# Scores of both kv heads issued in turn, and the projection of the 64 sample rows with high and low feature parts side by side

## What is computed

```python
xn = rmsnorm(x, p["attn_norm_w"])
proj = xn @ p["w_in"]                 # q, k, v, mq, mk, mv, mo, mi, mf, ga, gb
q = rmsnorm(q.reshape(B, T, N_KV_HEADS, G, HEAD_DIM), ...) * (HEAD_DIM ** -0.5)
k = rmsnorm(k.reshape(B, T, N_KV_HEADS, HEAD_DIM), ...)
...
s = jnp.einsum("bnqhgd,bnkhd->bnhgqk", q, k)     # per block of 128 queries: its own and the previous key block
...
p = jnp.exp(s - m)
den = p.sum(axis=-1, keepdims=True) + jnp.exp(sink - m)
return jnp.einsum("bnhgqk,bnkhd->bnqhgd", (p / den), v)
```

## Time and profile before

| | |
|---|---|
| median of 3 runs | 1626.4 us (1626.13 to 1628.06) |
| the profiled execution | 1630.05 us, span 1628.2 us |
| TensorE matmuls busy | 1465.9 us, 90% |
| VectorE busy | 986.0 us, 61% |
| ScalarE busy | 739.1 us, 45% |
| mean granted TensorE clock | 0.955 of full speed |
| `project`: first to last of its matmuls | 21.1 to 314.7 us |
| `mix_prompt`: its first gate matmul | 322.6 us |

### The profile page before, as it was taken

One profiled execution on the slowest core, in us unless ns is written; L12 is line 12 of the kernel. 1 busy time (PEld: TensorE's weight loads), 2 busy tenths in 40 slices (PEclk: granted clock), 3 DMA queues, 4 the chain that ended last, 5 costly groups with the idle time before them and its releaser, 6 DMA issues. The chain is left out here.

```text
span 1628.2 us, 22132 instructions
## 1 busy us (share of the span) xinstructions
PE 1465.9 (90%) x8287; PEld 1254.0 (77%) x8287; DVE 986.0 (61%) x1316; ACT 739.1 (45%) x869; POOL 203.8 (13%) x233
## 2 busy tenths in 40 slices
PE   6999999789999999789989947999999999999960
PEld 5999999788999999778868835777777777777740
DVE  4422311135555555657556665888888888888845
ACT  6321120134444444332132105777777777777732
POOL 2600000001111111200020002211111111111003
PEclk9999999889999999899999967999999999999985
DMA  6222228333333321646751055999999999999818
GB/s 219 74 74 74 73 77 259 104 109 96 96 95 95 95 89 54 168 136 179 229 224 71 33 219 183 382 385 403 390 393 388 401 395 389 388 400 397 311 64 326
DMA packets 135556, 347.54 MB, mean 213 GB/s; under 512 B 13528, under 2 KB 91804, under 8 KB 109824
## 3 DMA queue, kind: packets, MB, share of 16 engines
q1 hardware_dynamic: 125224, 312.11, 52.8%
q0 software_dynamic: 6160, 21.89, 4.4%
q10 hardware_dynamic: 4120, 12.85, 2.0%
HBM read 292.91 MB, written 54.89 MB: 214 GB/s over the span
## 5 line engine op out<-in xcount | busy, mean ns | idle before, releaser
L455 PE MATMUL pj<-w_hi,f_hi 128*128 128x352 f32 (+3 forms) x576 | 187.7, 326 | 4.7 <-ACTq L171 4.7
L456 PE MATMUL pj<-w_lo,f_hi 128*128 128x352 f32 (+3 forms) x576 | 187.1, 325 | 0.0
L457 PE MATMUL pj<-w_hi,f_lo 128*128 128x352 f32 (+3 forms) x576 | 186.8, 324 | 0.0
L2077 DVE TENSOR_TENSOR e_w_lo<-mixed,e_w_hi 128x2048 fp32r<-128x2048 f32 x64 | 145.7, 2296 | 11.7 <-ACT e_w_hi L2009 11.7
L2077 DVE TENSOR_TENSOR e_w_lo<-w_out,e_w_hi 128x2048 fp32r<-128x2048 f32 x64 | 143.5, 2283 | 0.0
L870 PE MATMUL gate_banks<-f_hi,wg_hi 128*128 128x364 f32 (+1 forms) x384 | 130.7, 340 | 10.3 <-PEq L93 7.6
L2009 ACT CAST e_w_hi<-mixed 128x2048 fp32r<-128x2048 f32 x64 | 120.2, 1906 | 37.7 <-PEq L93 21.2
L871 PE MATMUL gate_banks<-f_lo,wg_hi 128*128 128x364 f32 (+1 forms) x384 | 127.1, 331 | 0.0
L872 PE MATMUL gate_banks<-f_hi,wg_lo 128*128 128x364 f32 (+1 forms) x384 | 126.9, 331 | 0.0
L2009 ACT CAST e_w_hi<-w_out 128x2048 fp32r<-128x2048 f32 x64 | 121.7, 1902 | 1.7 <-PE e_up L2147 1.7
L455 PEld LDWEIGHTS pj<-w_hi,f_hi 128*128 128x128 f32 (+1 forms) x576 | 105.4, 183 | 7.4 <-ACTq L171 5.6
(11 more groups left out here) (496 smaller groups left out, 3393.8 us busy)
## 6 DMA issues: line engine op xcount, KB each, us to landing
w_out<-in_w_down_e SPq DMA_DIRECT2D x64, 1024.0 KB, 8.9
mixed<-in_w_gate_e SPq DMA_DIRECT2D x32, 1024.0 KB
mixed<-in_w_up_e SPq DMA_DIRECT2D x32, 1024.0 KB, 9.2
w_gate<-in_w_gate_e SPq DMA_DIRECT2D x32, 1024.0 KB, 7.6
w_up<-in_w_up_e SPq DMA_DIRECT2D x32, 1024.0 KB, 8.9
expert_rows<-e_y_rows ACTq DMA_DIRECT2D x32, 384.0 KB, 7.4
proj<-mixed SPq DMA_DIRECT2D x8, 1408.0 KB, 6.1
proj_tile<-proj SPq DMA_DIRECT2D x8, 1408.0 KB, 6.2
```

What stands on the lines that cost most here:

```text
L455: pe.matmul(banks[b][:r, :w], hi, w_hi[v][:, k, 0:w], start=(k == 0), stop=False)
L456: pe.matmul(banks[b][:r, :w], hi, w_lo[v][:, k, 0:w], start=False, stop=False)
L457: ins = pe.matmul(banks[b][:r, :w], lo, w_hi[v][:, k, 0:w], start=False, stop=(k == KD - 1))
L2077: dve.tensor_tensor(lo(i, u, j), raw(i, u, j), hi(i, step, j).bitcast(F32), ALU.subtract).then_inc(lo_ready[i], 1)
```

## The change

In `project` the sample tile gets a second copy of its features (`side`): per block k 128 stationary columns, the high part in the first 64 and the low part in the last 64. One matmul of it with the high weights gives high times high in the upper half of the bank's partitions and low times high in the lower half; the matmul of the high features with the low weights (64 columns) is added to the upper half as before. The two halves are added afterwards: ScalarE copies partitions 64 to 127 to `stage`, then VectorE adds partitions 0 to 63 (`add_sample`), frees the bank and counts `staged` up, for which `store` now waits. In `mix_prompt` the score matmuls alternate between the two kv heads, both counts of `sc_full` come at the end, and the waits for `mqT` and `mkT` stand in front of the first score.

```diff
+        side = [nc.alloc_sbuf_tensor_at("f_side0", [P, KD - 1, P], F32R, offset=nc.sbuf_base - 4 * (3 * D - 2 * T)),
+                nc.alloc_sbuf_tensor_at("f_side1", [P, 1, P], F32R, offset=S["mixed_at"] + 4 * (2 * half + 2 * T))]
...
-                    copy(stage[v][:r, t, :], banks[b][:r, :CW]).then_inc(done, 1)
+                    at = slice(TS, P) if t == NT else slice(0, r)
+                    copy(stage[v][:r, t, :], banks[b][at, :CW]).then_inc(done, 1)
...
-                    eng.wait_ge(done, per * cc + t // 2 + 1)
-                    eng.sem_inc(free[b], 1)
+                    if t < NT:
+                        eng.wait_ge(done, per * cc + t // 2 + 1)
+                        eng.sem_inc(free[b], 1)
+
+            def add_sample(dve, n):
+
+                cc, v = n // 2, n % 2
+                b = 3 * v + NT % 3
+                dve.wait_ge(staged[0][v], 5 * cc + 5)
+                dve.tensor_tensor(stage[v][:TS, NT, :], stage[v][:TS, NT, :], banks[b][:TS, :CW], ALU.add).then_inc(staged[1][v], 1)
+                if n == 0:
+                    dve.wait_ge(if_staged[0], 5)
+                    held = if_tok[:TS, NT, :].rearrange("p (g c) -> p g c", g=2)[:, :, 0:H]
+                    dve.tensor_tensor(held, held, banks[b][:TS, CW:CW + 2 * H].rearrange("p (g c) -> p g c", g=2), ALU.add).then_inc(if_staged[1], 1)
+                    dve.wait_ge(if_staged[1], 5)
+                dve.wait_ge(staged[1][v], 5 * cc + 5)
+                dve.sem_inc(free[b], 1)
...
                 def store(n):
                     cc, v = n // 2, n % 2
                     sp.wait_ge(staged[0][v], 5 * cc + 5)
-                    sp.wait_ge(staged[1][v], 4 * cc + 4)
+                    sp.wait_ge(staged[1][v], 5 * cc + 5)
...
                 def feat_hi(t, r):
                     act.wait_ge(featT_ready, t + 1)
-                    act.copy(feat(f_hi, t, r), f_tile[t % 2][:, :, 0:r]).then_inc(f_hi_ready, 1)
+                    ins = act.copy(feat(f_hi, t, r), f_tile[t % 2][:, :, 0:r])
+                    if t == NT:
+                        act.wait_ge(f_lo_ready, NT)
+                        for ks in (slice(0, KD - 1), slice(KD - 1, KD)):
+                            ins = act.copy(f_side(ks)[:, :, 0:TS], f_tile[t % 2][:, ks, 0:TS])
+                    ins.then_inc(f_hi_ready, 1)
...
                 def feat_lo(t, r):
                     dve.wait_ge(f_hi_ready, t + 1)
+                    if t == NT:
+                        for ks in (slice(0, KD - 1), slice(KD - 1, KD)):
+                            dve.tensor_tensor(f_side(ks)[:, :, TS:P], f_tile[t % 2][:, ks, 0:TS], feat(f_hi, t, r)[:, ks].bitcast(F32), ALU.subtract)
...
                     evacuate(dve, 1, dve.tensor_copy, n, 0 if n else 4)
+                    add_sample(dve, n)
                     if n < NCH - 2:
                         split_lo(n + 2)
...
+                    if t == NT:
+                        for k in range(KD):
+                            if k:
+                                pe.matmul(banks[b][:r, :w], f_hi[:, k, TP:T], w_lo[v][:, k, 0:w], start=False, stop=False)
+                            ins = pe.matmul(banks[b][:, :w], f_side(slice(k, k + 1)).rearrange("p o t -> p (o t)"), w_hi[v][:, k, 0:w], start=(k == 0), stop=(k == KD - 1))
+                            if k == 0:
+                                pe.matmul(banks[b][:r, :w], f_hi[:, k, TP:T], w_lo[v][:, k, 0:w], start=False, stop=False)
+                        ins.then_inc(full[b], 1)
+                        return
...
-                    for kv, X in enumerate((XA, XB)):
-                        if kv:
-                            pe.wait_ge(s["mqT_ready"], t + 1)
-                            pe.wait_ge(s["mkT_ready"], t + 1)
-                        hv = halves[kv]
-                        for g in range(G):
-                            for i, slot in enumerate((1 - u, u)):
-                                c = (2 * g + i) * P
-                                ins = pe.matmul(X[:, c:c + P], qT[hv, g, :], kT[slot][hv, :], start=True, stop=True)
+                    pe.wait_ge(s["mqT_ready"], t + 1)
+                    pe.wait_ge(s["mkT_ready"], t + 1)
+                    for g in range(G):
+                        for i, slot in enumerate((1 - u, u)):
+                            c = (2 * g + i) * P
+                            pair = [pe.matmul(X[:, c:c + P], qT[hv, g, :], kT[slot][hv, :], start=True, stop=True) for X, hv in zip((XA, XB), halves)]
+                    for ins in pair:
                         ins.then_inc(s["sc_full"], 1)
```

More of the change, by code:

```diff
@@ L158, in evacuate @@
                 cc, v = n // 2, n % 2
-                per, done = 5 - odd, staged[odd][v]
+                per, done = 5, staged[odd][v]
                 if cc:
@@ L164, in evacuate @@
                     eng.wait_ge(full[b], 3 * cc + t // 3 + 1)
-                    copy(stage[v][:r, t, :], banks[b][:r, :CW]).then_inc(done, 1)
+                    at = slice(TS, P) if t == NT else slice(0, r)
+                    copy(stage[v][:r, t, :], banks[b][at, :CW]).then_inc(done, 1)
                     if n == 0:
                         copy(if_tok[:r, t, :].rearrange("p (g c) -> p g c", g=2)[:, :, 0:H],
-                             banks[b][:r, CW:CW + 2 * H].rearrange("p (g c) -> p g c", g=2)).then_inc(if_staged[odd], 1)
+                             banks[b][at, CW:CW + 2 * H].rearrange("p (g c) -> p g c", g=2)).then_inc(if_staged[odd], 1)
                         eng.wait_ge(if_staged[odd], t // 2 + 1)
-                    eng.wait_ge(done, per * cc + t // 2 + 1)
-                    eng.sem_inc(free[b], 1)
+                    if t < NT:
[13 more added lines that the diff above has]
+                dve.sem_inc(free[b], 1)
             @block.sync
@@ L225, in feat, with f_side @@
                 return ap[:, :, t * P:t * P + r]
+            def f_side(ks):
+                return side[0][:, ks, :] if ks.stop < KD else side[1][:]
             @block.scalar
@@ L480, in _ @@
                 pe.wait_ge(if_staged[0], 5)
-                pe.wait_ge(if_staged[1], 4)
+                pe.wait_ge(if_staged[1], 5)
                 for t in range(NT):
@@ L2279, in build @@
         mixed, mixed_at = placed(ctx, "mixed", [P, KD * T])
-        S["mixed"] = mixed
+        S["mixed"], S["mixed_at"] = mixed, mixed_at
         S["x_hi"], S["x_lo"] = (nc.alloc_sbuf_tensor_at(f"mixed_{n}", [P, KD, T], F32R, offset=at) for n, at in (("hi", S["featT_at"]), ("lo", mixed_at)))
```

## The result

The changed kernel takes 1612.5 us (median of four, 1609.6 to 1615.5); the kernel before took 1627.2 beside it (median of four, 1626.1 to 1629.5). The ratio is 0.989, 95% interval 0.9875 to 0.991: some 15 us or 1.1% faster. The profiled executions are 1613.63 us against 1630.05: 16.4 less.

What follows compares the result with a forecast made beforehand. TensorE's matmul slots were taken to bound both stages. Projection 7.7 us plus scores 8.75 us gave 16.4 us: 1613.6 for the profiled execution, and 1610 us forecast because the median is 3.7 lower; range 1606 to 1617.

Steps and rivals of the forecast that it cites:

- rival A: Whole kernel: both parts work as predicted, 1610 us, own range 1607 to 1613; chance 0.78.
- Sample tile: Projection: 16 matmuls for 24 at unchanged pitch, saving 1.27 us in each of eight chunks, 10.2 us at most.
- Rival C: Sample tile: each switch of column width drains the array, up to 0.16 us; 1626 us, no change; chance 0.05.
- Features in front of the sample tile of chunk 0: Projection, chunk 0: extra copies and subtractions hidden before TensorE arrives, cost 0; without that cover up to 1.7 us.
- The add: Each chunk's end: 0.53 us, 0.6 with semaphore, hidden between chunks; lengthens the chain at the stage's end by 0.6.
- The wait in chunk 7: TensorE's wait behind the `wg` loads grows from 1.5 to about 3.4 us.
- The step that failed: Projection, chunk 7: longer wait swallows chunk 6's saving and loses 0.6 us for chunk 5's add; projection sum 7.7 us.
- wait in chunk 2: Projection: one of TensorE's two other waits, 3.2 us together, said to stay unchanged counted from a chunk's end.
- Scores: Prompt stage: all 16 matmuls pair, saving 1.25 us in each of seven tiles, 8.75 us; tile 0 gains 0.
- Rivals B: Prompt scores: row halves pair only in part, 1614 us, chance 0.06, or not at all, 1620 us, chance 0.06.
- D: Prompt scores: each switch of row half drains the array, 0.16 us each; 1639 us, slower; chance 0.04.
- Merge: Stage after the prompt tiles: untouched by the change, only starts sooner by the whole sum; own gain 0.

Runs made afterwards that it cites:

- second group: Changed kernel timed again, number of the last block loaded with bounds asserted, beside a kernel before of 1627.1 us: 1609.8 us, ratio 0.9888.
- version with the wait filled: Changed kernel plus sixteen matmuls with unused results in front of tile 3 of chunk 7: 1607.1 us, ratio 0.9869.
- moved `wg` loads: Kernel before with the two gate-weight loads ahead of the zeros in SP's queue: ratio 0.9964; timed again 1626.5 us, ratio 0.9989.
- projection part alone: Kernel before with only the projection's part of the change, old score loop kept: 1620.7 us, ratio 0.9951.
- blocks of four: Changed kernel with scores in blocks of four matmuls per kv head instead of one and one: 1616.0 us, single run.
- grouped columns: Changed kernel with sample-tile matmuls sorted by stationary width, two switches instead of fourteen: 1614.3 us, single run.
- version with the loads moved: Changed kernel with the two `wg` loads ahead of the zeros in SP's queue: 1606.1 us, ratio 0.9851.

## Why the prediction was right, and where it was not

The total held: 16.4 us less was foreseen for the profiled execution and 16.4 measured; the medians, 1612.5 and in the second group 1609.8, lie on both sides of the forecast 1610 and within rival A's own range. The mechanisms held; that the total agrees to the tenth is luck. The projection gave 2.65 us less than foreseen, the prompt stage 0.9 more, and the merge, of which nothing was foreseen, made up the rest.

- *Sample tile.* Foreseen 2.55 us long and 1.27 saved per chunk; measured 2.58 and 1.23. Rival C falls: at 0.3 us per switch the tile would last 4.8 us.
- *Features in front of the sample tile of chunk 0.* They were to take 0.8 us on ScalarE and 0.9 on VectorE, hidden; they take 0.71 and 0.96, VectorE has copied tile 5 out at 58.08, and TensorE goes from tile to tile every 0.16 us.
- *The add.* 0.51 us, foreseen 0.53. It lengthens the gap at the stage's end from 7.63 to 8.25 us, foreseen 0.6.
- *The wait in chunk 7.* Foreseen 3.4 us, measured 3.41, and 3.37 and 3.34 in the others.
- *The step that failed.* That wait was costed as elapsed time alone ("1.5 becomes 2.8 us", and the add of chunk 5 on top). The sum left out that TensorE's clock falls while it stands, and that the matmuls behind it then have the pitch of 1.2 GHz. From the end of the wait to the last matmul of the projection it is 24.38 us in the profiled execution of after, 24.29 in its second one, and 21.72 in the version with the wait filled: the slow clock cost 2.7 and 2.6 us, and the projection gave 5.05 us and not 7.7. Rows that were at hand showed it: the eight transposes take 1.97 us behind the 6.23 us wait of tile 0, and 1.04 us in tile 2, where there is none. The chain itself is as the prediction told it. That 7.7 less 2.7 gives just the 5.05 is luck too: this execution reached the first sample tile 0.58 us late (the second one of after did not), and from there on the projection saves 8.35 us without the slow clock, 0.65 more than foreseen. Some 0.3 of that is the shorter wait in chunk 2 (1.14 for 1.41), which the prediction had called unchanged; the rest is not traced.
- *Scores.* Foreseen 1.25 us for each of seven tiles, 8.75; measured 7.66 in six, 1.28 each, and 1.35 in tile 7. With 0.65 from tile 0, foreseen 0, the stage gave 9.66. That stretch holds two slow-clock starts and lies between 52.6 and 54.6 us over these profiles, so its share can't be put down to the change. Rivals B and D fall: every pair starts together, at the pitch that one stream had.
- *Merge.* Foreseen nothing, 1.8 us in the two profiles shown. The kernel before alone differs by 3.4 us there between two executions. It happens to fill part of the hole that the clock made.

What is still open: how much the moved `wg` loads give the kernel before in all. The two intervals do not quite meet (3.8 to 8.2 and 0 to 3.6 us); only the 1.8 us in the projection are shown.

## What to carry to other kernels

Cost a wait that grows on TensorE twice: the time it stands, and the matmuls behind it at the lower clock; look in the trace of before at what stands behind its long waits, and compare the mean of the same operation elsewhere. A saving ahead of a point that a DMA chain sets is not only lost, it can turn into such a wait, and reordering the queue that holds the load up (here two `dma_start` lines moved, 6 us) is then worth about as much as the whole cut was (the projection part alone, 6.4 us by the medians). Compare stages from a common instruction inside of them: the first microseconds of an execution scatter too. Matmuls that fill only half of the rows go out in turn, one of either half, and not in two streams.

## What the runs showed of the hardware

- Two matmuls with 64 contraction rows each, on partitions 0 to 63 and 64 to 127, run at the same time all along: 32 records in 1.78 us, starts at most 0.01 us apart. The Trainium skill, "TensorE: Matmul & The Clock Gate", Part 3, says the same of row groups. It also says that matmuls start in the order of the program; the rows here differ: with blocks of four, XB's record at 416.26 lies ahead of three of XA that were issued before it (416.37, 416.48, 416.59). The measurement decides. At each such seam, and at the one in the kernel before, the two streams overlap by three or four records; that the reach of the queue sets this number is a reading and not shown.
- Behind waits of 3.15 to 3.41 us the granted clock was 0.50 for 3 to 6 us in all five profiled executions that had such a wait and no filling (after twice, the projection part alone, the blocks of four, the grouped columns); behind the 1.51 us of the kernel before it was 1.00. Nearly the same wait cost 2.7, 2.6 and 1.3 us in three of them. The version with the wait filled has its four runs within 0.3 us and after has five within 3.6, but the version with the loads moved, which has neither the wait nor the slow clock there, has five within 4.7; that the scatter of the whole is made at this place is therefore not shown.
- A long wait is not the only thing that the clock falls behind. In the first profile of the kernel before with the moved loads it is 0.50 from 417.6 to 421.0 us, in the middle of the prompt stage, behind waits of only 1.28 and 0.39 us, and the six tile periods take 246.42 us for 244.92. None of the other thirteen profiles has this, and no run shows what sets it off. The windows (the first number behind POOL's is the clock):

```profile
413.00:417.60 4.60, 2.93 (x22) 2.46 (x20) 3.45 (x6) 1.94 (x4) 3.92 (x4) 1.00 0.85 281
417.60:421.00 3.40, 3.40 (x13) 3.40 (x13) 2.52 (x7) 0.63 (x1) 0.00 (x0) 0.50 0.20 57
```
